# Norm and residual chains between the layers: the wait behind the TensorE's jump, the root table, and the second stream's gate product

## The chip, the cores and the metric

The kernel runs on one core of a Trainium2 chip. Its engines are the TensorE (PE, matrix products into PSUM), the VectorE (DVE), the ScalarE (ACT, functions from tables), the GpSimd (POOL) and the SyncE (SP, which here only issues transfers). Each has its own instruction stream, and they meet at semaphores. The metric is the device time of one execution in microseconds; lower is better.

## The reference

One inference step of a two-layer trunk over two streams of 128 tokens by 1024 values: stream 0 (context) and stream 1 (noisy latents). Layer 0 mixes tokens by a bidirectional gated linear recurrence, layer 1 by differential attention; behind each mixer stands a mixture of 64 experts, 8 of them chosen for each token, and a shared expert. All is fp32. Around every sub-layer stands the part that this change is about:

```python
def modulate_in(x, g, shift, scale):
    return rms_norm(x, g) * (1.0 + scale) + shift
def residual_out(x, y, g, gate):
    return x + gate * rms_norm(y, g)
# for each layer i:
hp, hs = modulate_in(xp, ...), modulate_in(xs, ...)
yp, ys = mixer(hp), mixer(hs)              # 0: lru_mixer, 1: diff_attend and diff_out
xp, xs = residual_out(xp, yp, ...), residual_out(xs, ys, ...)
fp, fs = moe(modulate_in(xp, ...)), moe(modulate_in(xs, ...))
xp, xs = residual_out(xp, fp, ...), residual_out(xs, fs, ...)
```

`rms_norm(y, g)` is y divided by the root of the mean of its squares (plus 1e-6) over the 1024 values, times g.

## The kernel before

Every engine's program is written out by hand in one order, and semaphores named in `SEMAPHORES` join them. Nothing is scheduled by a planner. The norms have the numbers n = 0 (mixer of layer 0), 1 (MoE 0), 2 (attention) and 3 (MoE 1).

**A seam** is what lies between the last matmul of one sub-layer and the first of the next. Its steps, for each stream st:

- ACT, `rms_of_y`: squares of the result Y, which lies in four PSUM banks (two for each stream), summed along the row, then a root (`ACT.Sqrt`). Roots need another function table than the sigmoid and SiLU that the MoE uses, so an ACT_TABLE_LOAD stands before the first root.
- DVE, `residual_of`: reciprocal, then Y times that scalar times the gate `ggb` (L1550), then the addition to x (L1554), which counts up `x_new`.
- ACT, `rms_of_x`: squares of the new x (L1215) and root. DVE, `normed`: reciprocal and scaling (L1516).
- TensorE, `norm_turn`: 16 transposes (L670), four banks of four; ACT and DVE, `input_of`: copies out of PSUM with scale and shift into hT (L1226, L1525). For n = 1 and 3 ACT loads the sigmoid table ahead of these copies (`load_sigmoid`).

DVE does both streams' residuals before the first stream's scaling, as the code stands.

**The MoE** of a layer takes its experts in PASSES = 26 passes: two ahead, then three rounds of eight passes, of which the first two are a hardware loop and the last is written out. A pass gathers tokens by matmuls, multiplies by gate and up weights (`gate_up`), by down weights (`down`), and adds the result into Y (`scatter`, which counts up `scattered` once for each stream). Expert weights stream into four places of `ring` and one of W, refilled by SP as passes free them. What doesn't fit the fixed passes goes into extra pairs: `extra_pairs` reads a count from SBUF (`value_load`) and branches over the body when it is 0, and over the loop for further pairs when it is at most 2. The body stands twice in every engine's code. With these inputs layer 0 runs no extra pair and layer 1 runs one. Behind the extra pairs the TensorE runs a tiny matmul that counts up `y_done`, on which ACT's squares wait, and in layer 0 SP's loads of QKV blocks 0 and 1.

**Between the layers** SP loads the six blocks of the QKV weights, 2 MB each, into ring places 0 to 3 and again 0 and 1. It loads blocks 2 and 3 behind the last pass, then 0 and 1 behind y_done. ACT issues the transfers of the cached keys and values (L1452, L1453), behind x_new 4 and ahead of its squares of x; they are waited for behind QKV, before the keys are turned.

**The attention** runs a pipeline over eight units u in 11 steps: scores, maximum, exponentials on ACT (L1471, steps 0 to 7), products, copies (L1484) and squares (L1492) on ACT, and one root at the end (L1495).

Matmuls all have the helper's line L662, transposes by `eng.transpose` their own.

## Time and profile before

| | us |
|---|---|
| median of 3 runs | 1540.11 |
| lowest, highest | 1537.73, 1550.16 |
| the profiled execution | 1540.69 |
| its span | 1538.7 |
| TensorE busy | 1347.3 (88%) |
| DVE, ACT busy | 483.9 (31%), 356.3 (23%) |

The profiled execution's time includes 2.0 us around the span. Busy time counts neither register nor branch nor semaphore instructions: a TensorE that waits for its own instruction stream shows as idle with "issue" as the releaser. Times of rows are from the span's start. The first seam is the one behind MoE 0 (799 to 823 us), the second is in front of MoE 1 (985 to 998 us).

### The profile page before, as it was taken

What the parts mean: (1) busy time and instruction counts of PE and PEld (TensorE: products, weight loads), DVE (VectorE), ACT (ScalarE), POOL (GpSimd) and SP (SyncE); (2) the same over time, 40 slices, a digit from 0 to 9 for tenths busy, and PEclk for the clock granted to TensorE, in tenths of its full rate; (3) what the DMA queues carried; (4) which work ended last, traced back from release to release, by engine and by line L of the source; (5) the groups of instructions that cost most, each with busy time, mean ns of one, the idle gap of its engine ahead of it and who ended that gap; (6) DMA issues with size and microseconds to landing.
All of it is one profiled execution on the core that took longest, in us unless ns stands there. A gap on an engine that the chain in (4) does not pass through costs nothing.

```text
span 1538.7 us, 24283 instructions
## 1 busy us (share of the span) xinstructions
PE 1347.3 (88%) x9678; PEld 692.6 (45%) x9731; DVE 483.9 (31%) x1232; ACT 356.3 (23%) x713; POOL 10.7 (1%) x9
## 2 busy tenths in 40 slices
PE   5999979599998988999976987799999898889985
PEld 2777634364443433444423455364444343344432
DVE  2656500333223222223223226243322222223232
ACT  2157111221222111111222025222211121111221
POOL 2000000000000000000000000000000000000000
PEclk9999989699999999999997997899999999999998
DMA  9864967949999999999965322658999999999990
GB/s 359 264 233 165 350 239 267 406 187 359 420 420 420 420 420 420 421 420 420 420 231 190 109 83 82 271 225 332 420 421 420 419 421 421 420 420 421 420 388 30
DMA packets 104433, 506.83 MB, mean 329 GB/s; under 512 B 18633, under 2 KB 23302, under 8 KB 54406
## 3 DMA queue, kind: packets, MB, share of 16 engines
q1 hardware_dynamic: 102592, 501.32, 81.0%
q10 hardware_dynamic: 1414, 2.89, 0.5%
q8 instruction: 84, 1.38, 0.4%
q0 software_dynamic: 320, 1.06, 0.2%
q14 instruction: 23, 0.19, 0.0%
HBM read 503.13 MB, written 2.11 MB: 328 GB/s over the span
## 4 chain that ended last, share of the span: by engine, by line
PE 65%; DMA 22%; ACT 5%; DVE 4%; issue 2%; SPq 2%; ACTq 0%; DVEq 0%
PE PS L662 63%; DMA ring<-in_moe_w_up 18%; DMA ring<-in_mod_w 3%; SPq L496 2%; DMA diag<-in_shared_w_gate 1%; ACT W L1362 1%; DVE diag L1550 1%; DVE x L1554 1%; ACT W L1307 1%; PE PS L670 0%; PE PS L873 0%; DVE sst L2034 0%; SPq L490 0%; DVE diag L2052 0%; PE PS L1129 0%
## 5 line engine op out<-in xcount | busy, mean ns | idle before, releaser
L662 PE MATMUL PS<-ring,W 128*32 128x512 f32 (+3 forms) x2936 | 615.6, 597 | 5.0 <-DMA ring<-in_moe_w_up 3.0
L662 PE MATMUL PS<-W 128*128 128x128 bf16 (+5 forms) x3316 | 508.5, 368 | 30.3 <-DMA ring<-in_moe_w_up 16.1
L662 PEld LDWEIGHTS PS<-W 128*128 128x128 bf16 (+3 forms) x3318 | 229.1, 107 | 210.4 <-issue 163.3
L662 PEld LDWEIGHTS PS<-ring,W 128*32 128x32 f32 (+2 forms) x2936 | 175.6, 123 | 194.9 <-issue 183.8
L662 PE MATMUL PS<-W,junk 128*128 128x128 bf16 x848 | 117.0, 220 | 24.8 <-ACT W L1362 24.8
L1777 DVE COPY W<-PS 128x512 f32<-128x512 f32 x53 | 36.7, 692 | 277.6 <-PE PS L662 277.6
L1783 DVE TENSOR_TENSOR hT<-PS,hT 128x512 f32<-128x512 f32 x106 | 73.3, 692 | 154.4 <-ACT hT L1371 154.4
L662 PE MATMUL PS<-ring,hT 128*128 128x512 f32 x256 | 112.1, 600 | 2.4 <-issue 1.6
L662 PE MATMUL PS<-hT,W 128*128 128x512 bf16 x373 | 100.1, 385 | 13.9 <-issue 8.0
L1371 ACT CAST hT<-PS 128x512 bf16<-128x512 f32 x106 | 62.2, 586 | 197.7 <-PE PS L662 197.7
L1760 DVE SCALAR_TENSOR_TENSOR W<-W,PS 128x256 f32<-128x256 f32 x53 | 25.4, 480 | 237.0 <-ACT W L1358 237.0
L1358 ACT ACTIVATE W<-PS 128x256 f32<-128x256 f32 x53 | 20.4, 385 | 304.6 <-PE PS L662 304.6
L662 PE MATMUL PS<-hT,ring 128*128 128x256 f32 (+1 forms) x352 | 79.6, 410 | 10.2 <-ACT hT L1226 3.7
L662 PEld LDWEIGHTS PS<-W,junk 128*128 128x128 bf16 x848 | 63.2, 98 | 36.4 <-issue 24.8
L662 PEld LDWEIGHTS PS<-ring,hT 128*128 128x128 f32 x256 | 49.1, 193 | 64.6 <-issue 63.4
L662 PEld LDWEIGHTS PS<-hT,W 128*128 128x128 bf16 x424 | 37.4, 99 | 89.3 <-issue 48.6
L662 PEld LDWEIGHTS PS<-hT,ring 128*128 128x128 f32 (+1 forms) x352 | 66.1, 198 | 23.4 <-issue 10.8
L1788 DVE TENSOR_TENSOR W<-hT 128x1024 bf16<-128x1024 f32 x53 | 65.0, 1226 | 11.2 <-ACT hT L1373 11.2
L662 PE MATMUL PS<-ring,condT 128*32 128x384 f32 x512 | 53.1, 564 | 15.4 <-DMA ring<-in_mod_w 14.4
L1373 ACT CAST hT<-hT 128x1024 bf16<-128x1024 f32 x53 | 55.5, 1046 | 40.1 <-DVE hT L1783 40.1
L1366 ACT COPY W<-PS 128x512 f32<-128x512 f32 x53 | 31.1, 587 | 109.7 <-PE PS L662 109.7
L1362 ACT COPY W<-PS 128x256 f32<-128x256 f32 x53 | 19.7, 373 | 130.2 <-PE PS L873 130.2
(242 smaller groups left out, 882.8 us busy)
## 6 DMA issues: line engine op xcount, KB each, us to landing
ring<-in_moe_w_gate SPq DMA_DIRECT2D x106, 1024.0 KB, 19.7
ring<-in_moe_w_up SPq DMA_DIRECT2D x106, 1024.0 KB, 23.0
ring<-in_moe_w_down SPq DMA_DIRECT2D x106, 1024.0 KB, 21.6
ring<-in_mod_w SPq DMA_DIRECT2D x32, 1152.0 KB, 10.8
W<-in_moe_w_gate SPq DMA_DIRECT2D x24, 1024.0 KB, 15.4
W<-in_moe_w_up SPq DMA_DIRECT2D x24, 1024.0 KB, 17.9
W<-in_moe_w_down SPq DMA_DIRECT2D x24, 1024.0 KB, 20.0
ring<-in_mod_w SPq DMA_DIRECT2D x16, 768.0 KB, 13.5
```

Of the source, the lines that this page charges most:

```text
L496: eng.dma_start(v[:, i, :], w.rearrange("(p k) f -> p (k f)", p=P)).then_inc(done, 16)
L662: return eng.matmul(out, lhsT, rhs, start=first, stop=last, skip_group_check=True)
L1307: eng.activation(RAs[d][:, c, :], RAs[d][:, c, :], ACT.Exp, scale=la).then_inc(s.tanh_exp_done, 1)
L1358: eng.activation(sg, PS[:, 6, 0:F], ACT.Silu).then_inc(sg_.silu_ready, 1)
L1362: eng.copy(hT2.rearrange("p f n -> p (f n)"), PS[:, 7, 0:F]).then_inc(sg_.hT_ready, 1)
L1366: eng.copy(xg[:, 0:4, :].rearrange("p k n -> p (k n)"), PS[:, 6, :]).then_inc(sg_.xg_act, 1)
L1371: eng.copy(oparts[0][:, half * 512:(half + 1) * 512], PS[:, 4 + half, :]).then_inc(sg_.o_act, 1)
L1373: eng.copy(oparts[1], orest).then_inc(sg_.o_act, 1)
L1760: eng.scalar_tensor_tensor(out=hE.rearrange("p (c q) -> p c q", c=2), in0=sg.rearrange("p (q c) -> p c q", c=2), scalar=wslot[:, 0:1], in1 ...
L1777: eng.tensor_copy(xg[:, 4:8, :].rearrange("p k n -> p (k n)"), PS[:, 7, :]).then_inc(sg_.xg_dve, 1)
L1783: eng.tensor_tensor(orest[:, cols], PS[:, 4 + half, :], oparts[0][:, cols], ALU.subtract)\
L1788: eng.tensor_tensor(oparts[2], orest, oparts[1], ALU.subtract).then_inc(sg_.o_dve, 1)
```

## The change

It edits seams 1, 2 and 3, and the loads next to them.

- The matmul for y_done is gone. ACT's squares, and DVE, wait for `scattered` of the last fixed pass; in an extra pair ACT and DVE end with a small operation that waits for that pair's own scatters. The register loads of the count move ahead of the last passes on ACT and DVE, and ahead of the last round on the TensorE.
- `load_root`, a root of one column, is put behind the last pass's copies on ACT, and behind the last exponentials in attention. The table load goes to where it stands. In an extra pair the Silu and root tables are loaded again.
- In `residual`, for n = 1, 2 and 3, stream 1's product Y times gate is done first and without the norm's scalar; stream 1's residual is then one operation, scalar times that product plus x. ACT's square of stream 1 waits for the product (`y_scaled`).
- SP loads QKV blocks 0 and 1 when the last pass but one has freed their places, and blocks 2 and 3 behind x_new 3; layer 0's extra pairs use ring places 2 and 3. The cache transfers move from ACT's queue to POOL's.

```diff
@@ -542,7 +543,7 @@
 
                 xs = extra[L]
                 eng.wait_ge(s.xtable_ready, 2 * L + 2)
-                eng.wait_ge(s.down_done, 2 * (L + 1) * PASSES - 2)
+                eng.wait_ge(s.down_done, 2 * (L + 1) * PASSES - (0, 2)[L])
                 count = eng.value_load(xtab[0:1, X_COUNT:X_COUNT + 1], min_val=0, max_val=XITEMS)
 
                 def load_pair(i):
@@ -550,8 +551,9 @@
                         eng.wait_ge(xs.down_done, i * 2)
                     for q in range(2):
                         e = eng.value_load(xtab[0:1, bass.ds(i * 2 + (X_IDS + q), 1)], min_val=0, max_val=E - 1)
-                        load_gate_up(ring[:, q], a["moe_w_gate"][L, e], a["moe_w_up"][L, e], xs.loaded)
-                        load_down(ring[:, q], a["moe_w_down"][L, e], xs.loaded)
+                        at = ring[:, X_PLACE[L] + q]
+                        load_gate_up(at, a["moe_w_gate"][L, e], a["moe_w_up"][L, e], xs.loaded)
+                        load_down(at, a["moe_w_down"][L, e], xs.loaded)
 
                 extra_pairs(eng, count, load_pair)
 
@@ -617,16 +619,17 @@
             moe_loads(0, [("router", (s.wout_half, 1)), (4, (s.state_ready, 1)), (1, (s.mod_summed, 15)),
                           (3, (s.mod_summed, 16)), (0, (s.mixer_done, 2)), ("shared", (s.xT_turned, 8)),
                           (2, (s.logits_done, 1))])
-            extra_loads(0)
-            for j in (2, 3, 0, 1, 4, 5):
+            for j in range(6):
                 if j < 2:
-                    eng.wait_ge(s.y_done, 1)
+                    eng.wait_ge(s.down_done, 2 * PASSES - 2)
                 elif j < 4:
-                    eng.wait_ge(s.down_done, 2 * PASSES)
+                    eng.wait_ge(s.x_new, 3)
                 else:
                     eng.wait_ge(s.qkv_summed, 2 * (j - 3))
                 load_rows(N_QKV + j, a["attn_w_qkv"][0].rearrange("(k p) n -> p k n", p=P)
                           [:, :, j * 512:(j + 1) * 512], KD, 512)
+                if j == 1:
+                    extra_loads(0)
             for j in range(4):
                 eng.wait_ge(s.qkv_summed, 2 * (j + 3))
                 load_rows(N_WO + j, a["attn_w_o"][0].rearrange("(k p) n -> p k n", p=P)
@@ -651,6 +654,9 @@
             eng.wait_ge(s.state_copied, 1)
             eng.dma_start(new_state[0, 0].rearrange("d (c p) -> (d c) p", p=P), hlT[:, :])\
                .then_inc(s.caches_stored, 16)
+            eng.wait_ge(s.x_new, 4)
+            eng.dma_start(kv_c[:, 0], a["cache_k"][0, 0].rearrange("t h e -> t (h e)")).then_inc(s.cache_loaded, 16)
+            eng.dma_start(kv_c[:, 1], a["cache_v"][0, 0].rearrange("t h e -> t (h e)")).then_inc(s.cache_loaded, 16)
             eng.wait_ge(s.qkv_act, 6)
             eng.dma_start(new_k[0, 0].rearrange("t h e -> t (h e)"), qkv[:, 1, 0]).then_inc(s.caches_stored, 16)
             eng.dma_start(new_v[0, 0].rearrange("t h e -> t (h e)"), qkv[:, 2, 0]).then_inc(s.caches_stored, 16)
@@ -1081,24 +1087,22 @@
                              opens=i == 1)
                 with eng.Fori(0, ROUNDS - 1) as it:
                     one_round(it, False)
+                count = eng.value_load(xtab[0:1, X_COUNT:X_COUNT + 1], min_val=0, max_val=XITEMS)
                 one_round(ROUNDS - 1, True)
                 for st in range(NS):
                     scatter(s, (L + 1) * PASSES - 1, st, 1)
 
                 xs = extra[L]
-                count = eng.value_load(xtab[0:1, X_COUNT:X_COUNT + 1], min_val=0, max_val=XITEMS)
                 def extra_pair(i):
                     gather(xs, i, S[0])
                     turn_slots(xs, i * 4 + COLS, i, 0)
-                    gate_up(xs, i, lanes("A", 0), lambda: eng.wait_ge(xs.loaded, i * 96 + 96))
+                    gate_up(xs, i, lanes("A", X_PLACE[L]), lambda: eng.wait_ge(xs.loaded, i * 96 + 96))
                     turn_hidden(xs, i)
-                    down(xs, i, lanes("A", 0), lambda: None)
+                    down(xs, i, lanes("A", X_PLACE[L]), lambda: None)
                     for st in range(NS):
                         scatter(xs, i, st, 0)
 
                 extra_pairs(eng, count, extra_pair)
-
-                mm(PS[:, 7, 0:64], ident, ones[:, 0:64], True, True).then_inc(s.y_done, 1)
 
             moe(0)
 
@@ -1233,6 +1237,11 @@
                 act.settle()
                 act.keep(eng.activation(stat[:, 0, 0:1], epsc, ACT.Sigmoid))
 
+            def load_root():
+
+                act.settle()
+                act.keep(eng.activation(stat[:, 2, 0:1], epsc, ACT.Sqrt))
+
             def norm_in(n):
                 for st in range(NS):
                     rms_of_x(n, st)
@@ -1249,7 +1258,12 @@
 
             def rms_of_y(n, st):
 
-                eng.wait_ge(s.mixer_done if n % 2 == 0 else s.y_done, (st + 1, 1, 3, 2)[n])
+                if n % 2:
+                    eng.wait_ge(s.scattered, (n + 1) * PASSES)
+                else:
+                    eng.wait_ge(s.mixer_done, (st + 1, 0, 3)[n])
+                if n and st:
+                    eng.wait_ge(s.y_scaled, n)
                 act.settle()
                 act.keep(eng.activation(junk[:, :], Y[:, st, :], ACT.Square, accum_out=stat[:, 2, st:st + 1]))
                 act.settle()
@@ -1431,16 +1445,19 @@
                 group(0, False, True)
                 with eng.Fori(1, (PASSES - len(BODY)) // 2) as it:
                     group(it, False)
-                for it in range((PASSES - len(BODY)) // 2, PASSES // 2):
-                    group(it, it == PASSES // 2 - 1)
                 xs = extra[L]
                 eng.wait_ge(s.xtable_ready, 2 * L + 2)
                 count = eng.value_load(xtab[0:1, X_COUNT:X_COUNT + 1], min_val=0, max_val=XITEMS)
+                for it in range((PASSES - len(BODY)) // 2, PASSES // 2):
+                    group(it, it == PASSES // 2 - 1)
+                load_root()
                 def extra_pair(i):
                     copy_gathered(xs, i)
                     silu(xs, i)
                     copy_hidden(xs, i)
                     copy_down(xs, i)
+                    eng.wait_ge(xs.scattered, i * 2 + 2)
+                    eng.activation(stat[:, 2, 1:2], epsc, ACT.Sqrt)
 
                 extra_pairs(eng, count, extra_pair)
                 norm_out(n)
@@ -1448,9 +1465,6 @@
             moe(0)
 
 
-            eng.wait_ge(s.x_new, 4)
-            eng.dma_start(kv_c[:, 0], a["cache_k"][0, 0].rearrange("t h e -> t (h e)")).then_inc(s.cache_loaded, 16)
-            eng.dma_start(kv_c[:, 1], a["cache_v"][0, 0].rearrange("t h e -> t (h e)")).then_inc(s.cache_loaded, 16)
             norm_in(2)
             for j in range(6):
                 eng.wait_ge(s.qkv_summed, 2 * j + 1)
@@ -1475,6 +1489,8 @@
                         if i < 3:
                             act.keep(ins)
                     ins.then_inc(s.p_ready, 1)
+                if step == H:
+                    load_root()
                 if 2 <= step < H + 2:
                     u = step - 2
                     eng.wait_ge(s.wt_turned, u + 1)
@@ -1555,8 +1571,19 @@
 
             def residual(n):
 
-                for st in range(NS):
-                    residual_of(n, st)
+                if n % 2:
+                    eng.wait_ge(s.scattered, (n + 1) * PASSES)
+                else:
+                    eng.wait_ge(s.mixer_done, 3)
+                eng.wait_ge(s.ggb_ready, 4 * (n + 1))
+                eng.tensor_tensor(junk2[:, 1, :], Y[:, 1, :], ggb[:, 1, :], ALU.mult).then_inc(s.y_scaled, 1)
+                residual_of(n, 0)
+                eng.wait_ge(s.rms_out, 2 * n + 2)
+                eng.wait_ge(s.y_scaled, n)
+                dve.keep(eng.reciprocal(stat[:, 3, 1:2], stat[:, 3, 1:2]))
+                dve.settle()
+                eng.scalar_tensor_tensor(out=x[:, 1, :], in0=junk2[:, 1, :], scalar=stat[:, 3, 1:2], in1=x[:, 1, :],
+                                         op0=ALU.mult, op1=ALU.add).then_inc(s.x_new, 1)
 
             eng.wait_ge(s.vecs_turned, 1)
             for i, (n, at) in enumerate(ROW_TILES):
@@ -1974,10 +2001,11 @@
                 group(0, False, True)
                 with eng.Fori(1, (PASSES - len(BODY)) // 2) as it:
                     group(it, False)
+                xs = extra[L]
+                eng.wait_ge(s.xtable_ready, 2 * L + 2)
+                count = eng.value_load(xtab[0:1, X_COUNT:X_COUNT + 1], min_val=0, max_val=XITEMS)
                 for it in range((PASSES - len(BODY)) // 2, PASSES // 2):
                     group(it, it == PASSES // 2 - 1)
-                xs = extra[L]
-                count = eng.value_load(xtab[0:1, X_COUNT:X_COUNT + 1], min_val=0, max_val=XITEMS)
                 def extra_pair(i):
                     one_hots(xs, i * 4 + COLS, i, 0)
                     copy_gathered(xs, i)
@@ -1985,6 +2013,8 @@
                     hidden(xs, i)
                     rest_of_down(xs, i)
                     lowest_of_down(xs, i)
+                    eng.wait_ge(xs.scattered, i * 2 + 2)
+                    eng.tensor_copy(lam[:, 7:8], epsc)
 
                 extra_pairs(eng, count, extra_pair)
                 residual(n)
```

ACT's stream at the end of MoE 0, before: the last pass's copies, the count (TENSOR_LOAD W), the branch over the pair.

```order
L1371 CAST hT<-PS 128x512 [waits down_done] x2
L1373 CAST hT<-hT 128x1024 [waits o_dve]
L1438 TENSOR_LOAD W [waits xtable_ready]
L1438 ISA x2
L459 COMPARE_AND_BRANCH
```

And behind the pairs' code, where the branches land:

```order
L461 UNCONDITIONAL_BRANCH
L1254 ACTIVATE junk,stat<-PS 128x1024 [waits act_step,y_done]
L1256 ACT_TABLE_LOAD
L1256 ACTIVATE stat<-stat,con 128x1 [waits act_step]
L1254 ACTIVATE junk,stat<-PS 128x1024 [waits act_step,y_done]
L1256 ACTIVATE stat<-stat,con 128x1 [waits act_step]
L1452 DMA W<-in_cache_k 128x1024 [waits x_new]
L1453 DMA W<-in_cache_v 128x1024
```

Now the same places of ACT, with the first pair's code between them:

```order
L1387 CAST hT<-hT 128x1024 [waits o_dve]
L1243 ACT_TABLE_LOAD
L1243 ACTIVATE stat<-con 128x1 [waits act_step]
L460 COMPARE_AND_BRANCH
L1380 COPY W<-PS 128x512 [waits x0_gathered]
L1372 ACT_TABLE_LOAD
L1372 ACTIVATE W<-PS 128x256 [waits x0_gu_done]
L1376 COPY W<-PS 128x256 [waits x0_h_turned]
L1385 CAST hT<-PS 128x512 [waits x0_down_done] x2
L1387 CAST hT<-hT 128x1024 [waits x0_o_dve]
L1460 ACT_TABLE_LOAD
L1460 ACTIVATE stat<-con 128x1 [waits x0_scattered]
```

The table load has moved from behind the first square to ahead of the branch, and the count's load is gone from here.

DVE behind the pairs' code in layer 0, before:

```order
L1548 RECIPROCAL stat<-stat 128x1 [waits rms_out]
L1550 SCALAR_TENSOR_TENSOR diag<-PS,stat,ggb 128x1024 [waits dve_step]
L1554 TENSOR_TENSOR x<-x,diag 128x1024 [waits dve_step]
L1548 RECIPROCAL stat<-stat 128x1 [waits rms_out]
L1550 SCALAR_TENSOR_TENSOR diag<-PS,stat,ggb 128x1024 [waits dve_step]
L1554 TENSOR_TENSOR x<-x,diag 128x1024 [waits dve_step]
```

and now:

```order
L1579 TENSOR_TENSOR diag<-PS,ggb 128x1024 [waits ggb_ready,scattered]
L1564 RECIPROCAL stat<-stat 128x1 [waits rms_out]
L1566 SCALAR_TENSOR_TENSOR diag<-PS,stat,ggb 128x1024 [waits dve_step]
L1570 TENSOR_TENSOR x<-x,diag 128x1024 [waits dve_step]
L1583 RECIPROCAL stat<-stat 128x1 [waits y_scaled,rms_out]
L1585 SCALAR_TENSOR_TENSOR x<-diag,stat,x 128x1024 [waits dve_step]
```

One of stream 1's two large operations stands ahead of the first reciprocal, the other is merged with the addition.

## Rows read from the trace of the kernel before

**Rows 1.** The page's chain of waits by engine, as shares of the span.

```profile
PE 65%; DMA 22%; ACT 5%; DVE 4%; issue 2%; SPq 2%; ACTq 0%; DVEq 0%
```

**Rows 2.** Timeline, TensorE, first seam: start us, us, what, [idle before and its releaser].

```profile
799.08 0.59 PE L662 MATMUL PS<-W 128*128 128x512 bf16 x2
805.65 0.69 PE L662 MATMUL PS<-con 128*128 128x64 f32 x2 [5.98 <-issue]
818.01 3.68 PE L670 MATMUL PS<-con,diag 128*128 128x128 f32 x16 [11.66 <-DVE diag L1516]
823.33 84.38 PE L662 MATMUL PS<-ring,hT 128*128 128x512 f32 x192 [1.65 <-issue]
```

**Rows 3.** Timeline, ACT, first seam.

```profile
806.38 1.02 ACT L1254 ACTIVATE junk<-PS 128x1024 f32<-128x1024 f32 x1 [9.92 <-PE PS L662]
...
814.56 0.34 ACTq L1452 DMA_DIRECT2D W<-in_cache_k  x1
...
815.49 1.06 ACT L1215 ACTIVATE junk<-x 128x1024 f32<-128x1024 f32 x1 [5.06 <-DVE x L1554]
```

**Rows 4.** Timeline, DVE, first seam.

```profile
809.33 1.28 DVE L1550 SCALAR_TENSOR_TENSOR diag<-PS,stat,ggb 128x1024 f32<-128x1024 f32 x1
...
817.20 0.75 DVE L1516 TENSOR_SCALAR diag<-x,stat 128x1024 f32<-128x1024 f32 x1
```

**Rows 5.** Timeline, ACT, the last softmax steps.

```profile
942.37 0.60 ACT L1484 COPY diag<-PS 128x512 f32<-128x512 f32 x1
...
948.42 1.28 ACT L1495 ACT_TABLE_LOAD   x1
```

**Rows 6.** Timeline, TensorE, the last softmax steps.

```profile
944.30 2.91 PE L662 MATMUL PS<-W,diag 128*128 128x128 f32 x16
```

**Rows 7.** Timeline, ACT, second seam.

```profile
984.98 1.02 ACT L1254 ACTIVATE junk<-PS 128x1024 f32<-128x1024 f32 x1 [27.82 <-PE PS L662]
...
989.29 1.06 ACT L1215 ACTIVATE junk<-x 128x1024 f32<-128x1024 f32 x1 [1.54 <-DVE x L1554]
...
994.85 3.15 ACT L1226 ACTIVATE hT<-PS,modT,amod 128x128 f32<-128x128 f32 x8
```

**Rows 8.** Timeline, DVE, second seam.

```profile
986.66 1.28 DVE L1550 SCALAR_TENSOR_TENSOR diag<-PS,stat,ggb 128x1024 f32<-128x1024 f32 x1
987.98 1.23 DVE L1554 TENSOR_TENSOR x<-x,diag 128x1024 f32<-128x1024 f32 x1
...
991.96 0.75 DVE L1516 TENSOR_SCALAR diag<-x,stat 128x1024 f32<-128x1024 f32 x1
```

**Rows 9.** Timeline, TensorE, second seam.

```profile
992.77 3.68 PE L670 MATMUL PS<-con,diag 128*128 128x128 f32 x16 [7.83 <-DVE diag L1516]
998.09 3.32 PE L662 MATMUL PS<-hT,ring 128*64 128x256 f32 x16 [1.64 <-issue]
```

**Rows 10.** Timeline, ACT, extra pair and end.

```profile
1514.07 0.38 ACT L1358 ACTIVATE W<-PS 128x256 f32<-128x256 f32 x1 [8.96 <-PE PS L662]
...
1527.54 1.02 ACT L1254 ACTIVATE junk<-PS 128x1024 f32<-128x1024 f32 x1 [5.52 <-PE PS L662]
```

**Rows 11.** Timeline, TensorE, end.

```profile
1525.87 0.95 PE L662 MATMUL PS<-W 128*128 128x512 bf16 x2
...
1527.18 0.32 PE L662 MATMUL PS<-con 128*128 128x64 f32 x1 [0.31 <-issue]
```

**Rows 12.** Timeline, SP's queue, end.

```profile
1535.72 0.34 SPq L640 DMA_DIRECT2D out<-x  x1
```

**Rows 13.** Windows: stretch, length, busy us by engine, granted clock, DMA share, GB/s.

```profile
780.00:800.00 20.00, 16.25 (x120) 5.14 (x122) 5.87 (x11) 4.41 (x7) 0.00 (x0) 1.00 0.32 112
823.30:827.00 3.70, 3.67 (x5) 1.65 (x6) 2.06 (x11) 0.00 (x0) 0.00 (x0) 0.52 0.01 4
```

**Rows 14.** DMA issues: tile, queue, count, KB each, median us to landing.

```profile
out<-W POOLq DMA_DIRECT2D x2, 512.0 KB, 3.4
```

**Rows 15.** Timeline, TensorE, first pass of MoE 0's last round.

```profile
648.75 0.62 PE L662 MATMUL PS<-W 128*32 128x512 f32 x2 [1.48 <-DMA ring<-in_moe_w_up]
```

11 lines of the change are left out of this document (6 added, 5 removed).

## The prediction

> **What bounds the kernel now.** I read four views in this order. The chain of waits says how much of the span each engine holds: the TensorE has 65% of it and the weight transfers 22% [rows 1]. The kernel is thus two long MoE stretches, bound by matmuls or by the stream of expert weights, and between them short serial stretches. The change touches none of the long ones, so I went to the timelines of the serial ones: the seam behind MoE 0 [rows 2 to 4], the softmax's end [rows 5, 6], the seam in front of MoE 1 [rows 7 to 9] and the end of the program [rows 10 to 12]. The reader is to see the TensorE idle in each while ACT and DVE pass work to and fro; whatever shortens this passing moves all that follows, since all later loads and passes are released by it. The stretches of the windows view give clock and DMA traffic around the first seam [rows 13]. The last rows price what is moved elsewhere [rows 14, 15].
>
> **First seam, start.** The last scatter's matmul ends at 799.08 + 0.59 = 799.67. Then the TensorE is idle for 5.98 us with "issue" as the cause, and runs the tiny matmul of L1101 that signals y_done until 805.65 + 0.69 = 806.34 [rows 2]. The first square starts at 806.38, 0.04 later [rows 3]. I read the stall as the TensorE's instruction stream going over the extra-pair code, which layer 0 doesn't run; nothing else is late, as the last scatter had all its inputs. With the wait on `scattered` the square can start at 799.67 + 0.04 = 799.71, that is **6.67** earlier. The stall stays, but beside the chain: the TensorE is wanted next by the transposes, by my sum at 806.5, and even at its present pace it was through at 805.65.
>
> **First seam, chain.** From the first square to the first transposes it is now 818.01 - 806.38 = 11.63 [rows 2, 3]. In its place I put pieces, with the table already there: square to the first residual product 986.66 - 984.98 = 1.68 [rows 7, 8]; product and addition until 987.98 + 1.23 = 989.21, so 2.55 [rows 8]; to the square of x 0.08 [rows 7]; that square to the scaling 817.20 - 815.49 = 1.71, scaling 0.75, to the TensorE 0.06 [rows 2 to 4]. Sum 6.83, so transposes at 806.54, and this saves another 11.63 - 6.83 = **4.80**. It consists of the table load (first product at 809.33, 2.95 behind the square, where 1.68 do: 1.27), the second stream's part that the square of x no longer awaits (809.33 + 2.55 = 811.88 to 814.54: 2.66), and the cache transfers' issue on ACT, 815.49 - 814.56 = 0.93 [rows 3, 4], less 0.06 of small gaps. The added product of stream 1 (128x1024 from PSUM, at most the 1.28 of the form it replaces [rows 8]) runs 799.7 to 801.0, while the first product can start at 801.4 only, behind the first root: nothing is paid. ACT's second square, which now waits for it, has to follow that root anyway, near 801.1 by my estimate. Stream 1's x is done one operation behind stream 0's (806.5 - 1.2 = 805.3) and scaled by 805.4 + 1.71 + 0.75 = 807.9, when the TensorE, with 3.68 for 16 transposes, wants it at 808.4. If this cover went, up to 1.28 of the product would show.
>
> **What is moved past queues.** SP: QKV blocks 0 and 1 leave at the end of the last pass but one, near 780. Between 780 and 800 the DMA ran at 112 GB/s with a share of 0.32 [rows 13], so 350 if it were full: 4.2 MB need 12 us and are in by 792. Blocks 2 and 3 wait for x_new 3, at 804; they land near 816 and are wanted after two of six blocks of 84.38 / 6 = 14 us [rows 2], near 806.5 + 5.3 + 28 = 840. Cost 0, cover 24 us. POOL: the two cache transfers leave at 805.3 and are wanted behind QKV, near 811.8 + 84.4 + some 4 = 900; a POOL transfer of the same 512 KB landed in 3.4 us [rows 14]. The count's register load on the TensorE now stands before the last round: there it waited 1.48 us for weights [rows 15], more than a register load takes by any gap I see, so 0; bound 0 to 1. On ACT and DVE the same load lies in idle time.
>
> **Softmax.** The 1.28 table load at 948.42 stands in the chain [rows 5] and goes. It reappears with its root in front of the copy at 942.37, which started with no wait. That copy would end at 942.37 + 1.28 + 0.20 (my estimate for that root) + 0.60 = 944.45, and the matmuls that need it began at 944.30 [rows 6]: 0.15 lost. Net **1.1**; bounds 0 and 1.28.
>
> **Second seam.** It has no table load before its root and no jump, and gains by the second stream alone. The scaling of stream 0 waited for DVE, busy with stream 1, and began at 991.96; now the square at 989.29 + 1.71 allows 991.00, so 0.96 [rows 7, 8]. The TensorE starts at 991.81 in place of 992.77 and turns its last bank by 995.49. ACT's input copies now end at 994.85 + 3.15 = 998.00, and the router follows at 998.09 [rows 7, 9]; they would end half of 3.15 behind the last bank, 997.06. Net **0.9**.
>
> **End.** The last scatter ends at 1525.87 + 0.95 = 1526.82 and the square starts at 1527.54 [rows 10, 11]. Layer 1 runs an extra pair, so there is no long jump: 0.72 lies between. A root of one column on ACT and a copy on DVE now wait for that scatter; I take 0.4 of the 0.72 as saved, bounds 0 and 0.7. The Silu table that the pair must now load lies ahead of a silu that waited 8.96 us [rows 10]. The root table, 1.28, is loaded behind the pair's last cast, beside the scatter. The second stream is done 1.38 behind the first (0.10 + 1.28) where it was 2.66, so 1.28. The issue at 1535.72 [rows 12] comes 0.4 + 1.28 + 1.28, **2.95** earlier.
>
> **Sum.** 6.67 + 4.80 + 1.1 + 0.9 + 2.95 = 16.4. The profiled execution took 1540.69 (span 1538.7, 2 around it) and would take 1524.3. It stands 0.6 above the median of the three, 1540.11, so the forecast is **1523.7**.
>
> **A rule on the table load.** The row shows 1.28 for the load [rows 5], and the first seam with the load is 2.95 - 1.68 = 1.27 longer than the second without it [rows 3, 4, 7, 8]. The Trainium skill (ScalarE: Activation LUTs, What ACT_TABLE_LOAD costs) counts a drain of about 1.38 besides, 2.66 in all. By that the three loads off the path would save 4.1 more and the sum would be 20.5. The trace disagrees with the drain, by those 1.27, and I keep 1.28.
>
> **Rivals.**
> - *The clock moves the sum.* The first 3.7 us of QKV ran at a granted clock of 0.52, nearly the 1.2 GHz level, after 23.7 us in which the TensorE did little [rows 2, 13]. Now it idles 7 us in place of 18 before the transposes. If QKV then starts at 2.4 GHz, 1.8 more is won: 1521.9. If the clock comes back one such stretch later, 1.8 is lost: 1525.5. Both stay within the forecast's case.
> - *ACT and DVE pay for their jumps* (9 in 100). They now pass the extra-pair code on the path, before a square that nothing else delays. For: the TensorE's 5.98 for the same skip [rows 2]. Against: behind the pair in layer 1 the TensorE skipped the code of the further pairs with 0.31 idle [rows 11], and ACT's code there is some ten instructions to the TensorE's hundreds. Price: at most 5.98 at each of the two places, so 1529.7 for one and 1535.7 for both. The Trainium skill (Runtime: NRT & Kernel Launch, Instruction fetch mechanics) says that a taken branch out of the two resident blocks of instructions waits for a fetch. By it only a block's edge at the wrong place would bring this case about; no row shows where the edges lie.
> - *The TensorE's jump ends last after all* (7). It is through at 805.65 by the old start, and the margin is 0.9. If it took twice its 5.98, the transposes would start at 811.6, 5.1 late: 1528.8. Against: the DMA queues that the old jump met carried QKV weights, and now are empty from 791 to 804.
> - *What is won is absorbed* (6): a stretch behind a seam is bound by a transfer that isn't released earlier, and only the end's 2.95 is left: 1537.2. Against: every load of layer 1 waits for a signal of the chain.
> - *The cache transfers come late* (2), the case on the slower side. They stand on another queue, and the turning of keys waits for them. Price: what their landing exceeds 900 by, against 16.4 won, so slower from a landing behind 916, 111 us after issue at 805.3, where the row says 3.4 [rows 14]; a landing at 930 gives 1554. The Trainium skill (SBUF — State Buffer, SBUF: two separate sides) speaks against this edit: a transfer from POOL's queue cannot have its descriptors written while certain DVE operations hold a shared port. By it the landing slips by DVE's busy time, 5 us or so there, far inside the cover.
> - *The change doesn't do what it says* (2): the square still starts with the TensorE's return, by a wait I overlooked. Then 6.67 stays: 1530.4.
> - By the table rule above, 1 in 100: 1519.6.
>
> **How the numbers follow.** The forecast has 73 in 100, its spread some 2.5 us from the clock, the jump's margin, the 0 to 0.7 and 0 to 1.28 above, and the noise of medians. The range 1519 to 1532 takes in the clock's upside and all but the ends of the jump cases, and leaves out the absorbed, late and double-jump cases. A difference of 1% (15.4 us, so below 1524.7) is about what a measurement of this kernel can tell from none; the forecast lies 1.0 beyond it. Of its 73, about 52 fall below 1524.7; with the table case 53 in 100 are faster, 45 within 1%, 2 slower.
>
> **What would show it.** The first square of the first seam within 0.1 of the last scatter's end, with no table load behind it; the transposes 6.8 us after that end, and not led by "issue". QKV's first block with no wait on its weights. One table load ahead of the copy near 942 less the shift, none at the softmax's root. At the second seam the transposes 6.9 behind the matmuls' end where it is 7.8. At the end one stream's store 1.4 behind the other's. It is wrong if ACT or DVE sits idle with "issue" in front of the first square, if the transposes follow TensorE "issue" time, or if the MoE 1 stretch from router to last scatter, 1526.8 - 998.1 = 528.7, grows.

## The result, and the profile after

| | before | after | after / before, 95% interval |
|---|---|---|---|
| 10 runs each, median us | 1544.42 | 1532.04 | 0.9912 (0.9885 to 0.9940) |
| later, 17 and 6 runs | 1544.68 | 1529.27 | 0.9899 (0.9865 to 0.9933) |

The change makes the kernel 12 to 15 us faster, 0.9% in the first comparison and 1.0% in the second, one on each side of the 1% that the prediction took as its bound (it gave 53 in 100 to more, 45 to less). 1532.04 lies at the upper edge of its range (1519 to 1532), 8.3 above the forecast of 1523.7. The chain of waits keeps its shape against [rows 1]:

```profile
PE 67%; DMA 22%; ACT 5%; DVE 3%; issue 2%; SPq 2%; ACTq 0%; DVEq 0%
```

**First seam.** The timeline of the changed kernel's TensorE, against [rows 2] (start us, us, what, [idle before and its releaser]):

```profile
807.96 0.59 PE L668 MATMUL PS<-W 128*128 128x512 bf16 x2
815.42 3.52 PE L676 MATMUL PS<-con,diag 128*128 128x128 f32 x16 [6.86 <-DVE diag L1532]
820.60 1.96 PE L668 MATMUL PS<-ring,hT 128*128 128x512 f32 x4 [1.65 <-DVE hT L1541]
```

and of its ACT, against [rows 3]:

```profile
805.36 1.28 ACT L1243 ACT_TABLE_LOAD   x1
...
808.60 1.02 ACT L1268 ACTIVATE junk<-PS 128x1024 f32<-128x1024 f32 x1 [1.74 <-PE PS L668]
...
812.90 1.06 ACT L1219 ACTIVATE junk<-x 128x1024 f32<-128x1024 f32 x1 [1.54 <-DVE x L1570]
```

The last scatter ends at 807.96 + 0.59 = 808.55. The square starts 0.05 later where it was 6.71, the table is loaded ahead of it, and the transposes start 6.87 behind the scatter where it was 18.34. No idle time with "issue" stands in front of ACT's square or the transposes: TensorE's jump (its branch over the code of the extra pairs) is beside the chain, and ACT and DVE pay nothing for theirs. (Both wait for the scatter, 1.74 and 1.99 us long, so a jump of their own up to that length would be hidden.)

**Clock.** Two stretches of the windows view of the changed kernel (stretch, length, busy us of PE, PEld, DVE, ACT, POOL, granted clock, DMA share, GB/s), against [rows 13]:

```profile
820.60:824.30 3.70, 3.70 (x9) 1.78 (x10) 2.19 (x12) 0.00 (x0) 0.00 (x0) 1.00 1.05 397
951.50:955.20 3.70, 3.67 (x5) 1.61 (x6) 0.00 (x0) 0.00 (x0) 0.00 (x0) 0.50 0.00 0
```

QKV now starts at 2.4 GHz and does 9 matmuls in 3.7 us, where it did 5 at 0.52. But wo's product, which began at full clock before (1.00 in the window 957.2 to 960.9), begins at 1.2 GHz: at that place it takes back what it gave here.

**Softmax.** On ACT, against [rows 5], the table load stands ahead of an earlier copy:

```profile
938.04 1.28 ACT L1243 ACT_TABLE_LOAD   x1
...
939.45 0.57 ACT L1500 COPY diag<-PS 128x512 f32<-128x512 f32 x1
```

**Second seam.** TensorE, against [rows 9]:

```profile
951.53 29.54 PE L668 MATMUL PS<-ring,hT 128*128 128x512 f32 x64 [0.78 <-ACT hT L1516]
987.93 3.68 PE L676 MATMUL PS<-con,diag 128*128 128x128 f32 x16 [6.86 <-DVE diag L1532]
993.25 3.36 PE L668 MATMUL PS<-hT,ring 128*64 128x256 f32 x16 [1.64 <-issue]
...
999.04 1.99 PE L668 MATMUL PS<-hT,diag 128*128 128x256 f32 x8
```

The transposes come 6.86 behind wo's end (before 7.83). The product at 999.04 is the shared expert's first, and the chain of waits names its weights as the piece in front of it:

```profile
987.93 3.69 PE PS L676 x16
991.63 7.37 DMA diag<-in_shared_w_gate
999.04 6.30 PE PS L668 x22
```

**End.** ACT, against [rows 10]:

```profile
1517.45 1.28 ACT L1460 ACT_TABLE_LOAD   x1
1522.17 0.20 ACT L1460 ACTIVATE stat<-con 128x1 f32<-128x1 f32 x1 [3.44 <-PE PS L668]
1522.71 1.02 ACT L1268 ACTIVATE junk<-PS 128x1024 f32<-128x1024 f32 x1 [0.34 <-issue]
```

and SP's queue, against [rows 12]:

```profile
1526.96 0.36 SPq L641 DMA_DIRECT2D out<-x  x1
1528.35 0.34 SPq L643 DMA_DIRECT2D out<-x  x1
```

The last scatter ends at 1522.14. The square follows by 0.57 (before 0.72), the last store by 6.21 (before 8.90), and the two stores are 1.39 apart (forecast 1.38).

### The profile page after: what moved, and what is told of

It is laid out like the page before. It is cut to its first block, busy times and chain, and to the rows that moved or that the text cites. A ratio compares the mean times of both kernels' runs of the same rounds, so it can differ in the third digit from the quotient of the medians.

```text
span 1531.4 us, 24288 instructions
## 1 busy us (share of the span) xinstructions
PE 1356.6 (89%) x9674; PEld 695.7 (45%) x9727; DVE 484.3 (32%) x1233; ACT 359.3 (23%) x719; POOL 12.2 (1%) x11
## 3 DMA queue, kind: packets, MB, share of 16 engines
q8 instruction: 84, 1.38, 0.4%
## 4 chain that ended last, share of the span: by engine, by line
PE 67%; DMA 22%; ACT 5%; DVE 3%; issue 2%; SPq 2%; ACTq 0%; DVEq 0%
PE PS L668 65%; DMA ring<-in_moe_w_up 18%; DMA ring<-in_mod_w 2%; DMA diag<-in_shared_w_gate 2%; SPq L497 2%; PE PS L676 1%; ACT W L1376 1%; ACT W L1321 1%; PE PS L879 0%; DVE sst L2064 0%; DVE diag L1566 0%; ACT ring L1283 0%; PE PS L1133 0%; SPq L491 0%; DVE diag L2082 0%
## 5 line engine op out<-in xcount | busy, mean ns | idle before, releaser
L668 PE MATMUL PS<-hT,ring 128*128 128x256 f32 (+1 forms) x352 | 82.9, 421 | 10.2 <-ACT hT L1230 3.7
L668 PE MATMUL PS<-ring,condT 128*32 128x384 f32 x512 | 57.1, 599 | 16.0 <-DMA ring<-in_mod_w 15.0
L1815 DVE TENSOR_TENSOR W<-hT 128x1024 bf16<-128x1024 f32 x53 | 65.0, 1225 | 11.0 <-ACT hT L1387 10.9
## 6 DMA issues: line engine op xcount, KB each, us to landing
ring<-in_mod_w SPq DMA_DIRECT2D x32, 1152.0 KB, 10.3
```

Source lines behind the costliest of these rows:

```text
L668: return eng.matmul(out, lhsT, rhs, start=first, stop=last, skip_group_check=True)
L1815: eng.tensor_tensor(oparts[2], orest, oparts[1], ALU.subtract).then_inc(sg_.o_dve, 1)
```

## The experiments

All profiles are compared by the same marks, which are in each one's timeline. "Seam" is last scatter's end of MoE 0 to the first QKV matmul, "QKV" is from there to the first transpose of q and k (907.48 in the change), and "tail" is that scatter's end to the end of the span. The profile of before has a tail of 1538.70 - 799.67 = 739.03, that of the change 1531.4 - 808.55 = 722.85, so 16.2 less. But its span is only 7.3 shorter: the first mixer's output, in code that the change does not touch, ended at 271.7 before and at 280.3 after. That was the first thing to settle.

**Both kernels once more, no edit** (e1_before, e1_after).

> The kernel before once more, for the time at which the first layer's second chain begins (ScalarE's square L1254 behind the first mixer's output), which the change does not touch: 271.70 us in the profile of before, 280.36 in that of the change. Theory T (the work ahead of MoE 0 differs from execution to execution in both kernels, with the granted clock's low stretches): this time falls anywhere between about 270 and 281 us in this run and in the next, in no order of kernels. Rival R (the change slows that stretch by 8.7 us): here it is 271.7 within 1 us. By both, from MoE 0's last scatter to the end of the span it is 739.0 within 1.5 us.

> The changed kernel once more. Theory T: the first chain begins anywhere between 270 and 281 us; rival R: at 280.4 within 1 us. By both, from MoE 0's last scatter to the end of the span it is 722.9 within 1.5 us, 16.2 less than before.

Measured: the first chain starts at 280.7 in both, so R is out: the kernel before does this too. Over all 13 profiles it starts at 271.0 to 271.9 in four (two different kernels of the old order and two of the new), at 276.0 in one, at 279.8 to 280.9 in eight. In the stretch ahead of it the granted clock differs. The windows view of the profile of before, and then of its second profile:

```profile
145.00:170.00 25.00, 20.80 (x146) 15.35 (x145) 21.79 (x57) 7.41 (x18) 0.00 (x0) 1.00 0.73 282
```

```profile
145.00:170.00 25.00, 20.83 (x126) 13.85 (x125) 21.04 (x55) 8.50 (x22) 0.00 (x0) 0.80 0.61 235
```

and two pieces of the chain of waits that begin in the same stretch, of the one and then of the other:

```profile
149.00 7.69 PE PS L662 x60
157.56 25.68 PE PS L662 x168
```

```profile
150.86 10.58 PE PS L662 x60
162.32 27.30 PE PS L662 x168
```

The same products take 4.5 us longer where the clock is lower, half of the 9.0 by which the two executions differ when the first chain starts. The other half I have not traced.

The tail was 722.7 for the change, as expected, but 735.6 for the kernel before, not 739.0. Its TensorE:

```profile
808.31 0.59 PE L662 MATMUL PS<-W 128*128 128x512 bf16 x2
813.78 0.69 PE L662 MATMUL PS<-con 128*128 128x64 f32 x2 [4.88 <-issue]
826.14 3.42 PE L670 MATMUL PS<-con,diag 128*128 128x128 f32 x16 [11.66 <-DVE diag L1516]
831.20 1.10 PE L662 MATMUL PS<-ring,hT 128*128 128x512 f32 x2 [1.64 <-DVE hT L1525]
```

The jump costs 4.88 in place of 5.98, and its QKV starts at a granted clock of 1.00 in the window 831.2 to 834.9. So the saving by stretch, as forecast and in the two pairs of profiles:

| us saved | forecast | first pair | second pair |
|---|---|---|---|
| seam | 11.47 | 11.6 | 10.3 |
| QKV | 0 | 1.7 | 0.0 |
| QKV's end to wo's start | 1.1 | 1.2 | 1.0 |
| wo's product (27.75 to 29.55) | 0 | -1.8 | -1.8 |
| wo's end to the last scatter | 0.9 | 0.8 | 0.8 |
| last scatter to the end | 2.95 | 2.6 | 2.5 |
| sum (before rounding) | 16.4 | 16.2 | 12.9 |

The first pair meets the forecast by luck: what QKV gained and what wo's product lost, both by the clock and neither in the sum, nearly cancel.

**The start alone** (e1_start), on the kernel before. The count's loads and the pair's last operation are moved as in the change too, but that operation is a copy on ACT:

```diff
-                eng.wait_ge(s.mixer_done if n % 2 == 0 else s.y_done, (st + 1, 1, 3, 2)[n])
+                if n % 2:
+                    eng.wait_ge(s.scattered, (n + 1) * PASSES)
+                else:
+                    eng.wait_ge(s.mixer_done, (st + 1, 0, 3)[n])
...
+                    eng.wait_ge(xs.scattered, i * 2 + 2)
+                    eng.copy(stat[:, 2, 1:2], epsc)
```

> The kernel before with one part of the change alone: the squares behind a MoE wait for the last scatter in place of TensorE's extra product behind its jump, and the tail groups stand ahead of the extra pairs' branch as in the change, so that ScalarE and VectorE don't come late. Root tables, residual, cache transfers and the order of the loads stay as before. Theory (the start is 6.6 us of the first chain's 11.5): the square starts 0.05 us behind the last scatter (before: 6.3), the transposes end their wait 11.7 us behind it (before 18.3, change 6.87), and at the end of the program the square starts about 0.6 us behind the scatter (before 2.6). Rival (ScalarE and VectorE pay for a jump of their own once TensorE's no longer covers it): the square starts 3 to 6 us behind the scatter.

ACT in this kernel:

```profile
808.13 1.02 ACT L1257 ACTIVATE junk<-PS 128x1024 f32<-128x1024 f32 x1 [3.25 <-PE PS L662]
...
809.27 1.28 ACT L1259 ACT_TABLE_LOAD   x1
```

The square is 0.04 behind the scatter (808.09), the transposes 11.7, the tail 731.6: 4.0 less than the second profile of before and 7.4 less than the first. The theory holds, the rival (jumps of ACT's own) is out. The table load stands behind the first square, on the chain, as before. At the end of the program the square starts 0.29 behind the scatter, where 0.6 was expected; the 2.6 given there for the kernel before is a slip, it was 0.72.

**No table load in idle time** (e1_notable): the calls of load_root are removed, the pair's small root is a copy again.

```diff
-                    eng.activation(stat[:, 2, 1:2], epsc, ACT.Sqrt)
+                    eng.copy(stat[:, 2, 1:2], epsc)
...
-                if step == H:
-                    load_root()
```

> The change without its root-table loads in idle time: load_root is left out at its two places, and the extra pair's small root is a copy again. Theory: the load (1.28 us) comes back into each chain it was taken from: behind MoE 0 the transposes start 8.15 us behind the scatter in place of 6.87, behind the attention the same chain is as before since its table stays, the mixer's softmax has it again ahead of its root (QKV's end to the start of wo's product 45.3 in place of 44.05, of which wo's product gives some back, as it did in the kernel before, 27.75 against 29.55), and at the end of the program the last output is 1.28 later. Rival: the load in the softmax costs nothing in the end, since wo's product only waits for the clock otherwise: QKV's end to wo's end the same as in the change within 0.3.

Transposes 8.15 behind the scatter: the load costs 1.28 there and nothing besides. In the softmax it is back with 1.1, and then wo's product:

```profile
956.40:960.10 3.70, 3.68 (x9) 1.77 (x10) 0.00 (x0) 0.00 (x0) 0.00 (x0) 1.00 0.00 0
```

9 matmuls in 3.7 us at full clock against 5 in the change, 27.75 in all against 29.55. From QKV's end to wo's end this kernel is 0.7 *shorter* than the change: neither theory nor rival to the letter, the rival by its sense. The tail is 726.7, 3.8 more than the change: 1.4 in the seam, 1.6 in QKV (88.4 against 86.9, granted clock 0.57 at its start), -0.7 there, 0.6 in MoE 1, 0.9 at the end. The end gave less than the 1.28 of the load because the small operation in front of the square is a copy here and a root in the change. ACT with the copy:

```profile
1525.85 0.19 ACT L1459 COPY stat<-con 128x1 f32<-128x1 f32 x1 [4.94 <-PE PS L668]
1526.09 1.02 ACT L1268 ACTIVATE junk<-PS 128x1024 f32<-128x1024 f32 x1
```

The square starts 0.28 behind the scatter, 0.29 sooner than behind the root.

**The start undone, with an idle and with a busy DMA** (e2_jump_idle, e2_jump_busy). Both bring the extra product and the wait on it back; the second also has the old order of loads, and with it the old ring places of the extra pairs, whose code layer 0 skips.

```diff
+                mm(PS[:, 7, 0:64], ident, ones[:, 0:64], True, True).then_inc(s.y_done, 1)
...
-                    eng.wait_ge(s.scattered, (n + 1) * PASSES)
+                    eng.wait_ge(s.y_done, (n + 1) // 2)
```

```diff
-            for j in range(6):
+            extra_loads(0)
+            for j in (2, 3, 0, 1, 4, 5):
```

> The change, with the start of the chain undone: TensorE's small product behind the extra pairs' jump is back, and ScalarE's square and VectorE's product of the second stream wait for it; the order of the loads stays as in the change, so that SP has issued nothing for some 17 us when the jump is taken. Theory Q (the jump's own time depends on how busy the core's DMA engines are: in the change, where they lie idle there, TensorE's jump takes less than in the kernel before, though nothing waits for it): the square starts 2 to 3.5 us behind the last scatter, in place of 0.05 in the change and 6.7 in the kernel before, and the transposes' wait ends 9 to 10.5 us behind it (change 6.87). Rival (the jump costs the same in both orders): the square starts 6 us behind the scatter, the transposes 12.8.

> The same as the run before, but with the loads of QKV and of the extra items in the order of the kernel before, so that QKV's blocks 2 and 3 are on their way when TensorE jumps. Theory Q: the square starts 5 to 6.7 us behind the last scatter, the transposes 12 to 13.5. Rival (the order of the loads doesn't matter to the jump): the same as in the run before, whatever that is.

TensorE in the idle case, then the DMA queues between 802 and 806.5 us (queue and kind: packets, MB, share of 16 engines):

```profile
803.89 0.59 PE L668 MATMUL PS<-W 128*128 128x512 bf16 x2
806.26 0.43 PE L668 MATMUL PS<-con 128*128 128x64 f32 x2 [1.78 <-issue]
813.57 3.67 PE L676 MATMUL PS<-con,diag 128*128 128x128 f32 x16 [6.87 <-DVE diag L1534]
```

```profile
q8 instruction: 1, 0.02, 1.5%
```

and in the busy case, with the queues between 806 and 812.9:

```profile
807.78 0.59 PE L667 MATMUL PS<-W 128*128 128x512 bf16 x2
812.82 0.69 PE L667 MATMUL PS<-con 128*128 128x64 f32 x2 [4.44 <-issue]
820.37 3.67 PE L675 MATMUL PS<-con,diag 128*128 128x128 f32 x16 [6.86 <-DVE diag L1533]
```

```profile
q1 hardware_dynamic: 1386, 2.71, 104.2%
q8 instruction: 1, 0.02, 1.0%
```

The idle after the scatter is 1.78 or 4.44 by the order of the loads, the transposes 9.1 or 12.0 behind it. Theory Q holds (12.0 is the lower edge of what it gave). Around the jump stands exactly one packet of instructions, 16 KB: by itself, or among 1386 packets of weights that keep the 16 engines full. Its start can be found by narrowing the window, and it shows how the traffic acts:

| us from the last scatter's end | packet starts | packet ends | TensorE's next matmul |
|---|---|---|---|
| e2_jump_idle | -0.77 | 0.33 | 1.78 |
| e2_jump_busy | 1.86 | 2.96 | 4.45 |
| before, second profile | 2.30 | 3.40 | 4.88 |
| before | 3.40 | 4.49 | 5.98 |

The packet takes 1.1 in all four, and TensorE goes on 1.45 to 1.49 behind its end. What the transfers of weights lengthen is the time until the packet starts, by 2.6 to 4.2. That the packet is TensorE's own is my reading of this constant distance; the trace does not name its engine. The Trainium skill (Runtime: NRT & Kernel Launch, Instruction fetch mechanics) says that a taken branch to code outside the resident blocks waits for a DMA fetch of the target. The trace agrees, by the table above.

**The old residual** (e2_resid): one loop over the streams, product inside the chain, no wait on y_scaled.

```diff
-                eng.tensor_tensor(junk2[:, 1, :], Y[:, 1, :], ggb[:, 1, :], ALU.mult).then_inc(s.y_scaled, 1)
-                residual_of(n, 0)
...
+                for st in range(NS):
+                    residual_of(n, st)
```

> The change with the old residual: the product with the gate of the second stream stands in its chain again, behind its own root, and ScalarE's square doesn't wait for it. Theory: +1.3 us in each chain: behind MoE 0 the transposes start 8.1 us behind the scatter (6.87 in the change), behind the attention 7.8 behind wo's product (6.86), of which the second one is partly absorbed since shared gate's transfer ends last there; at the end of the program the last output is issued 7.5 us behind the scatter (6.2). Sum from MoE 0's scatter to the end: 722.9 + 2.6 to 3.5 us. Rival (the second stream isn't the one that ends last, the first is): nothing changes but the end of the program.

TensorE:

```profile
799.28 0.59 PE L668 MATMUL PS<-W 128*128 128x512 bf16 x2
807.70 3.68 PE L676 MATMUL PS<-con,diag 128*128 128x128 f32 x16 [7.83 <-DVE diag L1530]
```

1.0 at the transposes of each seam (1.3 was expected at the first) and 1.2 at the end; the rival is out. The tail is 726.2, 3.4 more than the change, and lies in the expected 2.6 to 3.5 partly by luck: 1.8 of it is QKV at a low clock again and 0.3 the attention, while MoE 1 was 2.0 shorter from router to last scatter, most of it at its beginning, where the router's 16 products took 1.95 against 3.36 in the change.

**Cache transfers on ACT** (e2_cache): the two transfers go from POOL's queue back to ACT's, ahead of its next square.

```diff
+            eng.wait_ge(s.x_new, 4)
+            eng.dma_start(kv_c[:, 0], a["cache_k"][0, 0].rearrange("t h e -> t (h e)")).then_inc(s.cache_loaded, 16)
+            eng.dma_start(kv_c[:, 1], a["cache_v"][0, 0].rearrange("t h e -> t (h e)")).then_inc(s.cache_loaded, 16)
```

> The change with the two cache transfers issued by ScalarE ahead of its next square, as before, in place of GpSimd. Theory: ScalarE issues them between x's update and its next square, which comes 0.85 us later (0.34 + 0.48 + a few hundredths in the kernel before, where the second stream's chain hid part of it), so the transposes start 7.7 us behind the scatter in place of 6.87; the rest stays. Rival (the issues wait long on ScalarE because the queue is busy): 2 us or more. Second rival (hidden behind VectorE's product of the other stream): nothing.

ACT:

```profile
814.18 0.41 ACTq L1465 DMA_DIRECT2D W<-in_cache_k  x1
814.64 0.54 ACTq L1466 DMA_DIRECT2D W<-in_cache_v  x1
...
815.28 1.06 ACT L1216 ACTIVATE junk<-x 128x1024 f32<-128x1024 f32 x1 [3.97 <-issue]
```

and TensorE:

```profile
817.80 3.67 PE L673 MATMUL PS<-con,diag 128*128 128x128 f32 x16 [9.30 <-DVE diag L1532]
```

9.3 behind the scatter, 2.43 more, and my 0.85 was wrong. The number fits the first rival, its reason does not: the issues take 0.41 and 0.54. What I had left out is the wait in front of them, for x_new 4. The square of the *first* stream's x stands behind it on ACT, so it waits for the *second* stream's x, one operation later. The square could start 4.35 behind the scatter in the change; here the first issue starts at 5.68 and the square at 6.78, so 1.33 is the wait and 1.10 the issues.

**Five rounds** of the change, of the start alone, and of a version that the profiles point to (e3_after, e3_start, e3_shared). The last is the change with this order of loads:

```diff
-                          (3, (s.mod_summed, 16)), (0, (s.mixer_done, 2)), ("shared", (s.xT_turned, 8)),
+                          ("shared", (s.xT_turned, 8)), (0, (s.mixer_done, 2)), (3, (s.mod_summed, 16)),
...
-                          (1, (s.mixer_done, 3)), ("shared", (s.xT_turned, 16)), (2, (s.logits_done, 2))])
+                          ("shared", (s.xT_turned, 16)), (1, (s.mixer_done, 3)), (2, (s.logits_done, 2))])
```

> The changed kernel once more, timed in five rounds against the kernel before. From MoE 0's last scatter to the end of the span the profiles so far gave 739.0 and 735.6 us for the kernel before and 722.8 and 722.7 for the change, and the time ahead of MoE 0 takes 271 to 281 us by the execution in both. Theory (only the seams differ): the difference of the medians lies between 12.9 and 16.2 us, ratio 0.9895 to 0.9917. Rival (something ahead of MoE 0 has become slower in the change and takes part of it back): under 12 us, ratio above 0.9922.

> The kernel before with the start of the chain alone changed (squares wait for the last scatter), now timed in five rounds. Profiled once it took 731.6 us from MoE 0's last scatter to the end of the span. Theory (its part of the whole is the 5.6 to 6.6 us of TensorE's jump and 0.4 at the end): 4.0 to 7.0 us less than the kernel before. Rival (the clock's low stretch behind the seam, which ended 17 us after it began both in this kernel and in the second profile of the kernel before, takes it back): under 2 us.

> The change with the shared expert's weights loaded ahead of those of experts 0 and 3 in layer 0 and of expert 1 in layer 1. In the profiles TensorE waits 9.5 us in the first of these places for a transfer that is issued at 289.2 (with the transposes' end) and lands 18.1 later, behind the experts' weights issued before it. Theory (it waits for the bytes ahead of it, and the experts passed over are wanted later than they then land): the wait goes to under 1 us, 8.5 to 9.5 us less than the change, and 0 to 0.4 more in layer 1; 1520.5 to 1524 in the median where the change has 1532. Rival (the DMA engines lie idle between the loads' release and the transposes' end, since SP waits for these with the experts behind it, and MoE 0 is bound by the stream of weights, which then runs that much later): 0 to 3 us less than the change, or some us more.

| | median us | against before, 95% interval |
|---|---|---|
| before (17 runs) | 1544.68 | |
| the change (6) | 1529.27 | 0.9899 (0.9865 to 0.9933) |
| the start alone (12) | 1539.02 | 0.9967 (0.9947 to 0.9988) |
| the change, shared weights first (6) | 1517.17 | 0.9840 (0.9807 to 0.9872) |

The change gains 15.4 and the start alone 5.7, both inside what the theory gave. The third is the best kernel, 27.5 faster than before and 12.1 faster than the change, more than the 8.5 to 9.5 expected (its lowest and highest runs, 1513.7 and 1522.7, lie 10.1 and 10.7 under the change's, and the mean of its six runs 10.9, so the medians overstate it a little). TensorE at MoE 0's beginning in the change (the profile of e3_after):

```profile
307.61 2.93 PE L668 MATMUL PS<-hT,diag 128*128 128x256 f32 x6 [9.68 <-DMA diag<-in_shared_w_gate]
```

and with the shared weights first:

```profile
287.88 0.56 PE L668 MATMUL PS<-con,W 128*128 128x64 f32 x4
288.27 1.95 PE L668 MATMUL PS<-hT,diag 128*128 128x256 f32 x8
```

No wait is left. The transfer lands 5.9 behind its issue in place of 18.1. From the mixer's end to the last scatter MoE 0 takes 516.7 against 528.3, 11.6 less: 9.7 of wait and 1.9 that I have not traced, though the first shared products above, 6 in 2.93 against 8 in 1.95, say that some of it is clock. In layer 1 the reordering gave nothing that the profile shows: the transfer landed 5.6 behind its issue in place of 7.4, but the shared product starts 17.96 behind wo's end where it was 17.97, and from the router to the last scatter it is 529.3 against 528.9.

## Why the prediction was right or wrong

- *First seam, start (6.67).* Right in mechanism and place; the size was one draw of a varying stall. The square comes 0.05 behind the scatter. What was removed cost 6.7 in one profile of the kernel before and 5.6 in the other, as the idle time with "issue" was 5.98 or 4.88. "The stall stays, but beside the chain" holds. That it would last as long was wrong, though without effect: with idle DMA engines it is short.
- *First seam, chain (4.80).* Right: 4.83 measured as start alone less the change, 11.70 - 6.87. Undone one at a time, the parts give 1.28 for the table, 0.96 for the residual, 2.43 for the cache transfers. The prediction divided it as 1.27, 2.66 and 0.93 and did not say which edit ends the 2.66, the second stream's wait. A good part of it hung on the transfers, which waited for that stream on ACT in front of the first one's square: of their 2.43, 1.33 is this wait, and the residual alone is worth 0.96. The expectation of 0.85 for e2_cache had missed it. The sum hides this; a kernel with the residual edit alone, which was not run, should show it.
- *Past the queues (0).* Right. QKV's first blocks show no wait, and from the first chain to MoE 0's last scatter it is 528.0 and 528.2 in the profiles of before and 528.2 in that of the change, so TensorE's moved register load costs nothing seen. The cache transfers on POOL land 7.3 and 8.3 behind their issue at 814.5 and 815.5, twice the 3.4 that the prediction took, but far ahead of 907.5, where they are wanted. The Trainium skill (SBUF — State Buffer, SBUF: two separate sides) says that a transfer from POOL's queue is held up while DVE runs certain operations. Against 6.5 and 8.8 on ACT's queue before, no such delay shows; whether an operation of that kind ran on DVE then, no row says.
- *Softmax (1.1).* The load left the chain as said (1.0 to 1.2), but wo's product began at 1.2 GHz and lost 1.8. That the one caused the other is likely, not shown: the product was fast in all five profiles with the load in the softmax's chain, and slow in six of the eight without it. The prediction priced the clock only at QKV's start, as a rival within the forecast. The same effect at the next place was its largest missing term.
- *Second seam (0.9).* Right, 0.96 at the transposes and at the router. In the profile of the change the shared weights' transfer then ends last, and 0.3 of it is lost on the way to the shared product. From the router to the last scatter the change takes 528.8 to 528.9 in its three profiles, the kernel before 528.7 in its two: the prediction's sign of being wrong, that this stretch grows, came by 0.1 to 0.2.
- *End (2.95).* 2.69 at the last store. The second stream's 1.28 and the table's 1.28 came; of the 0.72 behind the scatter only 0.15 went, not 0.4, since ACT has a further 0.34 of "issue" between the small root and the square. With a copy in place of the root (e1_notable, the start alone) 0.44 went.
- *Sum (16.4).* 16.2 in one pair of profiles and 12.9 in the other, 12.4 and 15.4 between medians. So the sum was a little too high, by the jump's length and the clock of QKV in the one profile it was read from, and by wo's product.
- *Base (1540.11).* The larger part of the miss: 4.3 of 8.3 in the first comparison, 4.6 of 5.6 in the second. The median of three runs was that much below the 1544.4 and 1544.7 of more runs. The time ahead of MoE 0 alone differs by up to 10 us from one execution to the next, so the median of three runs can lie several us off. Taken from 1544.4, the same sum gives 1528.0, 4.0 under the first median and 1.3 under the second.
- *Rivals.* The clock moved the sum, as feared, but at two places and with both signs. ACT and DVE paying for jumps, the jump ending last, late cache transfers: none occurred. *A rule on the table load:* leaving the idle-time load out moved the transposes by 1.28. The Trainium skill (ScalarE: Activation LUTs, What ACT_TABLE_LOAD costs) counts 2.66 with its drain; the trace disagrees.

Open: why wo's product starts at 1.2 GHz in some kernels (the change three times, e2_jump_idle, e2_resid, e2_cache: 29.5 to 30.2 us) and at 2.4 in others (before twice, the start alone twice, e1_notable, e2_jump_busy, e3_shared: 27.7 us), and what decides which way the first 280 us go.

## What to carry to other kernels

A wait for a signal that stands behind a branch also waits for that engine's instructions, and in these profiles they came later while weights were in transfer: signal from in front of the branch, or keep loads away from it. When a DMA issue sits on a compute engine's queue, price the wait in front of it, not only the issue. And before a saving of 1% is read from one profile, take a second one of the same kernel and compare stretch by stretch from a common mark, since untouched code alone moved by up to 9.9 us here, nearly as much as the change gained.

## What the runs showed of the hardware

- TensorE's jump over the same unused code left 1.78 us idle with the DMA engines nearly idle (share 0.02) and 4.44 to 5.98 with weights in transfer at a share near 1; one packet of instructions (16 KB) stood there in each of four profiles. It took 1.1 us in all, started 0.77 ahead of the scatter's end or 1.86 to 3.40 behind it, and TensorE went on 1.45 to 1.49 behind its end.
- The same instructions ran at 2.4 GHz in one execution and partly at 1.2 in another (1.00 and 0.80 on average between 145 and 170 us of two profiles of the kernel before), and the chain behind the first mixer started at 271.7 and 280.7; the products that begin in that stretch account for 4.5 of these 9.0.
- QKV took 86.9 us when it began at full clock and 88.4 to 89.9 otherwise, wo's product 27.75 or 29.5 to 30.2. In the change the chain ahead of wo's product is 1.0 to 1.2 shorter and the product 1.8 longer; that one causes the other was not shown.
- A root table load of 1.28 us, taken from idle time back into the first seam's chain, lengthened it by 1.28 and nothing besides. With a one-column copy instead of a one-column root in front of it, ACT's square started 0.28 behind its signal instead of 0.57.
